# Hybrid attention and SSD trunk: the last early weight slice split ahead of h, and a head's last `ada` part moved behind the next head's softmax

## The reference

```python
for i in range(DEPTH):                       # DEPTH = 2
    norm_w, ada_w, ada_b, mixer = layers[i]
    mod = silu(c) @ ada_w + ada_b            # ada_w: 2048 x 6144
    shift, scale, gate = split(mod)
    mod_c = silu(c_ctx) @ ada_w + ada_b
    shift_c, scale_c, gate_c = split(mod_c)
    h = rms_norm(x, norm_w) * (1 + scale) + shift
    hc = rms_norm(ctx, norm_w) * (1 + scale_c) + shift_c
    y, yc = mixer(h, hc)                     # na_mixer: q, k, v, z = t @ w_in
    x, ctx = x + gate * y, ctx + gate_c * yc
return rms_norm(x, final_norm_w)
```

## Time and profile before

| | us |
|---|---|
| median of 3 runs | 2072.31 (2070.05 to 2072.87) |
| the profiled execution, its own time | 2073.99 |
| its span, first to last instruction | 2072.1 |
| PE busy | 2016.3 (97%) |
| DVE busy | 1464.6 (71%) |
| ACT busy | 967.8 (47%) |
| POOL busy | 673.7 (33%) |
| mean granted TensorE clock | 0.99 |

### The profile page before, as it was taken

One profiled execution on the slowest core, in us unless ns is written; L12 is line 12 of the kernel. 1 busy time (PEld: TensorE's weight loads), 2 busy tenths in 40 slices (PEclk: granted clock), 3 DMA queues, 4 the chain that ended last, 5 costly groups with the idle time before them and its releaser, 6 DMA issues.

```text
span 2072.1 us, 31012 instructions
## 1 busy us (share of the span) xinstructions
PE 2016.3 (97%) x10458; PEld 1676.1 (81%) x10458; DVE 1464.6 (71%) x2076; ACT 967.8 (47%) x1398; POOL 673.7 (33%) x568
## 2 busy tenths in 40 slices
PE   5999999999999999999999999999999999999998
PEld 3567888888888888878878888888888888888886
DVE  5238777778777777773348878787878787787544
ACT  3145444445445444553355445445444545456443
POOL 1026666666656565635100111111212111110011
PEclk8999999999999999999999999999999999999999
DMA  9996666666676666655353554454454645556654
GB/s 352 323 278 142 175 183 179 166 166 180 175 178 180 169 175 176 164 140 164 102 152 100 148 153 129 135 152 127 136 155 110 166 116 147 139 150 198 226 183 154
DMA packets 422706, 349.23 MB, mean 169 GB/s; under 512 B 13600, under 2 KB 366464, under 8 KB 422016
## 3 DMA queue, kind: packets, MB, share of 16 engines
q1 hardware_dynamic: 397552, 273.43, 45.6%
q0 software_dynamic: 19968, 70.26, 14.0%
q10 hardware_dynamic: 5136, 4.89, 0.7%
HBM read 344.21 MB, written 4.33 MB: 168 GB/s over the span
## 4 chain that ended last, share of the span: by engine, by line
PE 85%; DVE 7%; DMA 3%; ACT 2%; issue 2%; SPq 1%; POOL 0%; DVEq 0%; ACTq 0%; POOLq 0%
PE bank L373 22%; PE bank L377 21%; PE bank L375 21%; DMA arena<-in_na_ada_w_dram 3%; PE bank L2305 3%; PE bank L2307 2%; PE bank L2306 2%; DVE w_lo L357 2%; PE bank L2109 1%; PE bank L2243 1%; PE bank L2224 1%; DVE arena L1649 1%; PE bank L2238 1%; PE bank L2024 1%; PE bank L1997 1%
## 5 line engine op out<-in xcount | busy, mean ns | idle before, releaser
L373 PE MATMUL bank<-act_hi,w_hi 128*128 128x512 f32 (+1 forms) x2448 | 905.3, 370 | 10.6 <-DVE w_lo L357 6.1
L377 PE MATMUL bank<-act_hi,w_lo 128*128 128x512 f32 (+1 forms) x2448 | 888.4, 363 | 0.0
L375 PE MATMUL bank<-act_lo,w_hi 128*128 128x512 f32 (+1 forms) x2448 | 887.7, 363 | 0.0
L357 DVE TENSOR_TENSOR w_lo<-arena,w_hi 128x2048 fp32r<-128x2048 f32 x184 | 437.5, 2378 | 205.7 <-ACT w_hi L353 147.9
L373 PEld LDWEIGHTS bank<-act_hi,w_hi 128*128 128x128 f32 x2448 | 462.7, 189 | 95.9 <-issue 14.5
L377 PEld LDWEIGHTS bank<-act_hi,w_lo 128*128 128x128 f32 x2448 | 462.3, 189 | 73.4
L375 PEld LDWEIGHTS bank<-act_lo,w_hi 128*128 128x128 f32 x2448 | 463.1, 189 | 68.5
L620 POOL TENSOR_TENSOR acc<-acc,arena 128x512 f32<-128x512 f32 x224 | 331.4, 1479 | 125.2 <-ACT arena L858 116.0
L353 ACT ACTIVATE w_hi<-arena 128x2048 fp32r<-128x2048 f32 x138 | 263.8, 1912 | 83.7 <-PE bank L2307 70.3
L858 ACT ACTIVATE arena<-arena,cond_c 128x512 f32<-128x512 f32 x256 | 171.3, 720 | 269.8 <-POOL acc L620 153.6
L1416 DVE SCALAR_TENSOR_TENSOR arena<-arena,cond_c 128x512 f32<-128x512 f32 x240 | 253.1, 1055 | 61.8 <-DMA arena<-in_ssd_ada_w_dram 40.6
(11 more groups left out here) (253 smaller groups left out, 2162.4 us busy)
## 6 DMA issues: line engine op xcount, KB each, us to landing
arena<-in_ssd_w_in_dram SPq DMA_DIRECT2D x81, 1024.0 KB, 6.0
arena<-in_na_w_in_dram SPq DMA_DIRECT2D x58, 1024.0 KB, 7.1
arena<-in_ssd_ada_w_dram POOLq DMA_DIRECT2D x96, 512.0 KB, 4.1
arena<-in_na_ada_w_dram SPq DMA_DIRECT2D x64, 512.0 KB, 8.1
arena<-in_ssd_w_out_dram SPq DMA_DIRECT2D x32, 1024.0 KB, 5.1
arena<-in_na_ada_w_dram POOLq DMA_DIRECT2D x32, 512.0 KB, 4.2
arena<-in_na_w_out_dram SPq DMA_DIRECT2D x16, 1024.0 KB, 6.3
arena<-cs_scr SPq DMA_DIRECT2D x64, 256.0 KB, 5.3
```

Of the source, the lines that this page charges most:

```text
L357: nc.vector.tensor_tensor(w_lo[:, n0 % 2, :], raw[slot], w_hi[:, n0 % 2, :].bitcast(F32), ALU.subtract).then_inc(s_lo, 1)
L373: nc.tensor.matmul(out[:, 0:cols], hi[:, w], act_hi3[:, k, 0:cols], start=(k == 0), stop=False)
L375: nc.tensor.matmul(out[:, 0:cols], hi[:, w], act_lo3[:, k, 0:cols], start=False, stop=False)
L377: mm = nc.tensor.matmul(out[:, 0:cols], lo[:, w], act_hi3[:, k, 0:cols], start=False, stop=(k == KT - 1))
```

## The change

Three edits. A list `BETWEEN` moves slice 7: ACT rounds it between the copy of the last block's sums and that block's h, and DVE makes its rest between the full-precision and the low half of h(14). POOL's first two `ada` loads are issued behind h(15) and no longer ahead of h(14). DVE's part 7 of a head leaves the end of that head's turn and stands in the next turn, between `normalise` and `ada_sums`; the last head's part 7 follows the loop. ACT's and POOL's orders in the heads stay as they are.

```diff
+BETWEEN = (None, None, None, None, 7)
@@ GpSimd, load phase
             for k in range(KT):
                 if k in FIRST_K:
                     pool.wait_ge(s_mod, FIRST_K.index(k) + 1)
-                if k == KT - 2:
-                    load_ada(0, None, True)
-                    load_ada(1, None, True)
                 if k >= 3:
                     pool.wait_ge(s_h, k - 2)
                 nc.gpsimd.tensor_scalar(hx[k % 3][:, LAT:TOK], xn_t[:, k, LAT:TOK], gain_a[:, 1, k:k + 1],
                                         mod_a[:, 0, 1, k:k + 1], ALU.mult, ALU.add).then_inc(s_hxp, 1)
+            load_ada(0, None, True)
+            load_ada(1, None, True)
@@ ScalarE, load phase
                 nc.scalar.activation(rows_a[:, c % 2, 0:nk * P], bank[2][:, 0:nk * P], ACT.Copy).then_inc(s_rows, 1)
+                if BETWEEN[c] is not None:
+                    first_hi(BETWEEN[c])
                 act.wait_ge(s_mod, c + 1)
                 act.wait_ge(s_xn0, KT)
                 for k in range(k0, k0 + nk):
                     h_high(k)
-                if BEHIND[c] is not None:
+                if BEHIND[c] is not None and BETWEEN[c] is None:
                     first_hi(BEHIND[c])
@@ VectorE, load phase
                     done = h_full(k)
+                    if k == k0 and BETWEEN[c] is not None:
+                        first_lo(BETWEEN[c])
                     step.wait(done)
@@ VectorE, ada_part
-                dve.wait_ge(s_gin[l % 2], 16 * (l // 2 + 1) if first else t8.i * 64 + (16 * (l // 2 + 1) - 64))
+                dve.wait_ge(s_gin[l % 2], 16 * (l // 2 + 1) if first else
+                            t8.i * 64 + (16 * (l // 2 + 1) - 64 + 64 * t8.base))
...
-                            dve.wait_ge(s_gd, l if first else t8.i * 8 + (l - 8))
+                            dve.wait_ge(s_gd, l if first else t8.i * 8 + (l - 8 + 8 * t8.base))
@@ VectorE, head
                 normalise(l3)
+                ada_part(7, l1)
                 ada_sums(i - 2, z_th)
...
-                for l in range(6, 8):
-                    ada_part(l, t1)
+                ada_part(6, t1)
@@ VectorE, first_heads and behind the loop
-                for l in range(6, 8):
-                    ada_part(l, none)
+                ada_part(6, none)
...
             with step.loop(2, HEADS, 14) as i:
                 head(Turn(i, 1), Turn(i, 4))
+            ada_part(7, Turn(HEADS - 1, 1))
```

## The result

The change makes the kernel slower: 2079.65 us median of 7 runs (2077.8 to 2081.39) against 2072.31 of the kernel before (7 runs, 2069.43 to 2072.99), a ratio of 1.0038 with a 95% interval of 1.0029 to 1.0047. The forecast was 2083 us. The profiled execution after took 2079.8 us, with a span of 2077.8; that of before had a span of 2072.1 us.

A forecast was written before the change was run, and what follows sets the result against it. PE, 97% busy, was taken as the bound, with a ring of DVE, ACT and POOL work right behind. The lag of +6.0 us by i = 15 plus +4.6 at the loop's end gave +10.6: 2083 us, range 2066 to 2096.

The forecast's parts named there:

- lead of the scores, turn 2: After block 4's pause goes and PE's wait for `v_t`, PE runs 3.5 us ahead of the kernel before.
- ring, one turn: DVE, ACT and POOL work from one gate of z to the next: 50.3 us, over PE's 49.5.
- start of head 2's last tile: Head 2: PE waits 3.1 us for the tile but starts it at 221.0 instead of 225.3, -4.3 us.
- thirteen heads from that start: Head 2 to i = 15: PE follows turns of 50.3 us instead of 49.51, +10.3 us.
- loop's end, from the start of head 15's last tile: ACT's high halves of o stand behind products (7), DVE's `o_low` follows and PE waits: +4.6 us.
- the rest of the program: Behind the loop's end PE is full again and only carries the lag: 0 us more.
- edit (2)'s charge: Head 1: the later `ada` loads delay ACT's copies, so PE may wait up to 0.8 us for `v_t`.
- Part 7 and POOL's queue: In each head the bias load waits behind part 7: 9.4 us after the gate instead of 3.3, products (2) at 24.6.
- (b): Heads: the chain beside PE isn't the limit, both pauses are won, -7.4 us: 2065 us, chance 0.14.
- (a): Heads: turns stay within 49.8 us, so PE waits only in head 2: 2070 to 2076 us, chance 0.20.
- (c): Load phase: slice 7 lands late, the first pause partly returns, up to 4.3 us: 2083 to 2086, no separate chance.
- (d): Heads: every pause drops PE's clock, costing about 0.9 us a head at most: 2095 us, chance under 0.05.

The follow-up runs named there:

- e9: Kernel before with only slice 7 moved; the two `ada` loads and part 7 stay in their old places: 2067.93 us, ratio 0.9985.
- e10: Changed kernel with POOL's bias load ahead of `load_ada(1)` and the first two `ada` loads back in their old place: 2067.79 us, ratio 0.9985.
- e3: Changed kernel with two POOL lines exchanged, the bias load ahead of `load_ada(1)`: 2068.64 us, ratio 0.9988.
- e8: Kernel before with one wait added on POOL, for the last head's part sums ahead of `load_ada(1)`: 2112.51 us, ratio 1.0196.
- e2: Kernel before with only part 7 moved behind `normalise`, load phase as before: 2077.79 us, ratio 1.0032.
- e4: Changed kernel with part 7 right behind the softmax, ahead of the split and `normalise`: 2085.23 us, ratio 1.0065.
- e7: Changed kernel with the bias load ahead of `load_ada(1)` and SyncE's 1 MB weight load held until products (2) are done: 2098.3 us, ratio 1.0135.
- e6: Changed kernel with SyncE's 1 MB weight load held until products (2) are done: 2083.0 us, ratio 1.0062.
- e1: Kernel before with slice 7 and the first two `ada` loads moved, part 7 still at the head's end: 2068.88 us, ratio 0.9988.
- e5: Changed kernel with part 7 right behind the softmax and SyncE's 1 MB weight load held until products (2) are done: 2072.47 us, ratio 1.0005.

## Why the prediction was right

The direction, its cause and its place held; the total came out 3.3 us high, with terms off on both sides that partly cancel, and that part of the closeness is luck. By its own steps, counted from block 4's copy (in us; below the first two rows a minus is time won against before):

| term | forecast | measured |
| --- | --- | --- |
| lead of the scores, turn 2 | 3.5 | 3.15 |
| ring, one turn | 50.3 | 49.97 |
| start of head 2's last tile | -4.3 | -3.4 |
| thirteen heads from that start | +10.3 | +5.9 |
| loop's end, from the start of head 15's last tile | +4.6 | +4.6 |
| the rest of the program | 0 | +1.1 |
| sum of the last four | +10.6 | +8.2 |

*Block 4, part (1) and (2).* Right. The wait of 2.69 us is gone, and short ones have come, for `v_t` (0.22 us where up to 0.8 was allowed) and of 0.63 us in head 1. e9 and e10 point the way of edit (2)'s charge, within the noise.

*Head 2.* This step failed in part. The forecast let the gate of z start 50.25 us behind the copy and `normalise` end 6.93 us behind the gate, as before, so that the pause of 2.31 us would go. The gate came at 50.99, `normalise` ended at 191.81, 8.1 us behind it, and 1.60 us of pause stayed. The row at 186.94 shows the second part: split 1 took 3.35 us where it takes 2.28 in later turns (338.54 us), and it ended 2.16 us behind the end of POOL's two sums, nearly its own length. For the last tile this didn't count. It was ready 35.4 us behind the gate (35.5 forecast), so 3.4 of the 4.3 us of lead were left, and 0.7 of the missing 0.9 is the later gate. PE waited 1.93 us for the tile and not 3.1. The clock behind it was 0.62, which takes (1 - 0.62) x 4.5 = 1.7 us: the scores of turn 3 came only 1.67 us sooner than before. The forecast had charged nothing for this, and rightly so in the end: at 320.27, in turn 4, PE waited for its last tile's split again (0.15 us), so the ring would have taken these 1.7 us anyhow.

*Part 7 and POOL's queue.* The step on which the forecast rested, and it held: bias at +9.92 in most turns (9.4 forecast), mask at +17.2 in the mean of turns 3 to 14 (17.4), `load_ada(2)` issued at +19.0 to 20.6, in the mean +19.6 (19.7), products (2) at +24.3 (24.6). In five of these twelve turns they wait for POOL's sum, in the others for the load, so these two ends lie as close as forecast. That the mask fits so well is luck: the bias load left 0.5 us late and took 7.2 us and not 8.2, and 9.4 + 8.2 would have been 17.6. e3 and e8 show the cause from both sides: with the bias load out of the queue's wait the loss vanishes, and a wait in the queue alone brings it back and more.

*The tile and the gate.* From the products (2) to the end of the tile's split it took 10.5 us (10.9), giving +34.8 (35.5). The step from the products (2) to (3) is 4.2 us in most turns, where it was 4.5 in turn 3 before. From the split to the next gate it took 15.1 (14.8; the 0.3 us that I took off weren't there), and this 15.1 stood in e2, e4, e7 and e8 too, but not in e6. The ring was thus 0.3 us too long in the forecast, and thirteen turns make 4.3 us of that: the largest error of the sum. From the start of head 2's last tile (219.22) to that of head 15's (868.65) thirteen heads took 649.4 us after and 643.5 before: +5.9, as 13 x (49.97 - 49.51) = 6.0 says. The measured ring lies at the lower end of the forecast's own 49.9 to 51.4. Its upper figures don't follow from its terms: a bias load of 9.1 us adds 0.9 and a load (2) of 7.4 adds 2.5, which gives 51.2 to 52.8 and not 51.4 to 52. And a wait in each head, as forecast, isn't what the profile lists: behind head 2 it has four up to head 15, 1.22 us the longest, though the scores lie up to 51.0 us apart.

*Behind the loop.* The high halves of o did stand behind the last products, and PE waited for `o_low`: 2.81 us, longer than the 1.42 before.

```profile
885.23 0.77 PE L374 MATMUL bank<-act_hi,w_hi 128*128 128x512 f32 x1 [2.81 <-DVE act_lo L1527]
```

```profile
885.00:889.00 4.00, 3.77 (x9) 2.63 (x10) 4.00 (x6) 4.00 (x9) 2.42 (x3) 0.57 1.04 304
```

From the start of head 15's last tile to PE's last wait at the loop's end, 1.27 us for `w_lo` (901.57, before 896.97), it took 4.6 us more than before. e3, whose ring isn't the bound, has only +0.9 us behind its last scores: that term too belongs to the ring. The 1.1 us left lie behind 901.57, in work that the change doesn't touch. From that wait to the end it is 1176.2 us here and 1175.1 before, but 1176.4 in e1 and 1175.2 in e7 as well, so I take it as spread.

*The rivals.* (b) is in kind what e3 shows: with the bias load out of the wait the ring isn't the limit; of (b)'s 7.4 us it gained 2.7. (a) was near in its ring (49.8 against 49.97) but not in its time: it let PE wait in head 2 only, while what the ring has over 49.51 us came back in every head, 5.9 us in all. (c) didn't occur; ACT didn't wait for a weight load at L804. (d) didn't occur as a whole: pauses of 0.56 and 1.22 us kept a clock of 1.00. In head 2, though, a pause of 1.93 us did not. No run was made for the 0.3 to 0.7 us that the forecast names for a first sum that meets part 1.

## What to carry over

When a step is moved later, walk down the in-order queue of every engine that waits for it, and ask for each instruction behind the wait whether it needs it; here exchanging two lines on GpSimd gave back all 11 us, while moving the step itself earlier cost 5.6 more. When a second chain stands within 1% of the bound, as here with 49.34 against 49.51 us, whatever lengthens it is paid once per turn. And never move a large transfer, or hold it back with a wait, without listing which small transfers leave just behind its new place: here those that left 0.5 to 1.8 us behind it took 2.2 to 3.6 us longer to land than one that left alone (6.2 to 7.6 against 4.0 us).

## What the hardware showed that I had not expected

**A 512 KB load just behind a 1 MB load lands after it.** The time from issue of the `ada` load to the products that use it, by how far it leaves behind SyncE's 1 MB weight load: 0.5 us behind, 7.7 us (e7); 0.9 behind, 7.6 (before, 353.44 and 354.30 us); 1.8 behind, 6.3 (e4); 3.2 behind, 4.7 (changed kernel); 1.7 ahead of it, 4.4 (e5, load 3). In the first four the products began 8.0 to 8.5 us after the *weight load's* issue, whenever the small load left itself, and the small load landed 1.2 to 1.4 us behind the large one. The DMA queues of the changed kernel from 351.2 to 359.4 us (packets, MB, share of 16 engines), the weight load in q1 and `load_ada(2)` in q0:

```profile
q1 hardware_dynamic: 2064, 1.05, 49.4%
q0 software_dynamic: 172, 0.55, 21.0%
```

In the kernel before, whose small load leaves at 354.30, the queues from 358 to 359 and from 359 to 360 us:

```profile
q1 hardware_dynamic: 614, 0.31, 108.5%
q0 software_dynamic: 3, 0.01, 3.0%
...
q0 software_dynamic: 81, 0.33, 85.6%
q1 hardware_dynamic: 122, 0.06, 22.4%
```

The small load has far fewer packets and yet moved none up to 358 us, until the large one was nearly through; the one of e5 that left alone at 351.20 had its first packets in the second us. So it stood behind the large load. The Trainium skill (DMA: Bandwidth & Descriptors, "Queues, rings and completion order") has each DMA engine take packets from its queues in turn. By that rule the small load would be through long before the large one; the trace doesn't agree, unless the page and the profile count packets differently. Why the engines serve the large load first was not tried.

**The clock.** In the changed kernel pauses of PE of 0.56, 1.22 and 1.60 us left the granted clock at 1.00 (the full level of 2.4 GHz); those of 1.93 and 2.81 us were followed by windows with a mean of 0.62 and 0.57, mostly at the level of 1.2 GHz. The other traces don't make a rule of this: 1.87 us was followed by 0.58 (e3, 882 to 886 us), but 2.53 us by 1.00 (e7, 219.9 to 224 us), 2.68 by 1.00 (e2, 142.1 to 146) and 2.71 by 1.00 (e8, 695.9 to 700). Between two pauses of nearly equal length that costs 1.7 us or nothing at the next scores, so an estimate of one pause has a step in it here, and one trace doesn't say on which side it falls.

**A DVE subtraction beside POOL.** Split 1 (128x2048) took 3.35 us in head 2 beside POOL's sums and 2.28 us in a turn where POOL waited. The forecast had seen this only from POOL's side (3.34 against 1.30 us for the first sum). It works both ways: the one that began second took longer, the split by 1.1 us, the sum by 2.0. In head 2 it is 1.1 us of the pause that stayed.
